# Folding 40 of 48 adaLN weight tiles on VectorE, with one partition sum on TensorE for each group of eight

## The reference

```python
def adaln(cond, w, b):
    m = jax.nn.silu(cond) @ w + b
    return jnp.split(m[..., None, :], 6, axis=-1)
# per layer: adaln(c, w_ada[l], b_ada[l]) for the latents, adaln(c_ctx, w_ada[l], b_ada[l]) for the context
# w_ada[l] is (1024, 6144)
```

## Time and profile before

| | |
|---|---|
| time, median of 3 runs | 1704.29 us (1699.11 to 1709.53) |
| span of the profiled execution | 1699.1 us |
| TensorE busy | 1617.3 us, 95% |
| VectorE busy | 522.5 us, 31% |
| ScalarE busy | 316.4 us, 19% |
| 48 adaLN tiles on TensorE (L1033) | 55.5 us |

### The profile page before, as it was taken

How to read it: one execution, slowest core, us unless ns; L and a number is a source line. 1 busy time by engine, 2 the same in 40 slices (tenths; PEclk the granted TensorE clock), 3 DMA queues, 4 the chain that set the end, 5 groups by cost and what they waited for, 6 DMA issues and landing times.

```text
span 1699.1 us, 21403 instructions
## 1 busy us (share of the span) xinstructions
PE 1617.3 (95%) x9009; PEld 987.5 (58%) x9009; DVE 522.5 (31%) x1217; ACT 316.4 (19%) x715; POOL 64.8 (4%) x68
## 2 busy tenths in 40 slices
PE   5999998999999999989999989999999998899987
PEld 2665644744444436854546556786678887555543
DVE  1232365522332212441211115345534314211112
ACT  2121234211111100110101013234312201100001
POOL 0000000000000000020000013000000000100000
PEclk8999999999999999999999999999999999999999
DMA  9564412232424348179999995422123466999996
GB/s 368 191 223 149 149 38 82 56 112 90 170 87 173 136 139 307 61 242 398 420 393 407 393 375 193 126 94 75 38 97 127 135 236 267 346 393 387 399 383 264
DMA packets 118863, 370.52 MB, mean 218 GB/s; under 512 B 6722, under 2 KB 83580, under 8 KB 96236
## 3 DMA queue, kind: packets, MB, share of 16 engines
q1 hardware_dynamic: 109516, 344.70, 54.4%
q0 software_dynamic: 4400, 13.69, 2.4%
q10 hardware_dynamic: 4848, 10.73, 2.0%
HBM read 356.40 MB, written 12.69 MB: 217 GB/s over the span
## 4 chain that ended last, share of the span: by engine, by line
PE 83%; DMA 5%; DVE 4%; ACT 2%; SPq 2%; issue 2%; another core or an unknown queue 1%; POOL 1%; ACTq 0%; DVEq 0%; POOLq 0%
PE ps L1223 15%; PE ps L1363 14%; PE ps L1096 11%; PE ps L1099 9%; PE ps L1020 8%; PE ps L1240 7%; PE ps L1381 6%; PE ps L1033 3%; DMA ring<-in_w_exp_gate 3%; SPq L852 2%; PE ps L1131 1%; PE ps L1126 1%; PE ps L1353 1%; PE ps L1406 1%
## 5 line engine op out<-in xcount | busy, mean ns | idle before, releaser
L1223 PE MATMUL ps<-hT,ring 128*128 128x512 f32 (+1 forms) x768 | 262.2, 491 | 1.4 <-ACT arena L1650 1.4
L1096 PE MATMUL ps<-hT,ring 128*128 128x512 f32 (+1 forms) x544 | 210.3, 540 | 0.0
L1223 PEld LDWEIGHTS ps<-hT,ring 128*128 128x128 f32 x768 | 142.4, 190 | 115.3 <-issue 105.9
L1099 PE MATMUL ps<-ring,hT 128*128 128x256 f32 (+1 forms) x832 | 174.5, 367 | 5.1 <-DVE arena L1926 4.0
L1099 PEld LDWEIGHTS ps<-ring,hT 128*128 128x128 f32 x832 | 147.4, 191 | 35.9 <-issue 18.7
L1096 PEld LDWEIGHTS ps<-hT,ring 128*128 128x128 f32 x544 | 101.4, 191 | 98.2 <-issue 93.2
L1240 PE MATMUL ps<-arena,ring 128*128 128x512 f32 (+1 forms) x384 | 133.4, 487 | 0.0
L1363 PE MATMUL ps<-ring,arena 128*64 128x256 f32 (+2 forms) x928 | 118.2, 378 | 8.3 <-DMA ring<-in_w_exp_gate 3.0
L1363 PE MATMUL ps<-arena 128*64 128x256 f32 (+2 forms) x1008 | 99.6, 355 | 2.7 <-DMA arena<-in_w_exp_up 1.7
L1240 PEld LDWEIGHTS ps<-arena,ring 128*128 128x128 f32 x384 | 72.2, 190 | 51.6 <-issue 46.7
L1363 PEld LDWEIGHTS ps<-ring,arena 128*64 128x64 f32 (+2 forms) x928 | 68.0, 136 | 55.3 <-issue 36.0
(11 more groups left out here) (265 smaller groups left out, 1531.8 us busy)
## 6 DMA issues: line engine op xcount, KB each, us to landing
ring<-in_w_in SPq DMA_DIRECT2D x54, 1024.0 KB, 6.3
ring<-in_w_ada SPq DMA_DIRECT2D x48, 1024.0 KB, 7.1
arena<-in_w_exp_down SPq DMA_DIRECT2D x18, 2048.0 KB
arena<-in_w_exp_up SPq DMA_DIRECT2D x15, 2048.0 KB, 25.4
ring<-in_w_exp_down SPq DMA_DIRECT2D x14, 2048.0 KB, 24.4
ring<-in_w_exp_gate SPq DMA_DIRECT2D x12, 2048.0 KB, 24.3
ring<-in_w_exp_up SPq DMA_DIRECT2D x12, 2048.0 KB, 24.9
hT<-in_w_exp_gate SPq DMA_DIRECT2D x10, 2048.0 KB, 24.9
```

The costliest lines, as they stand in the source:

```text
L1096: last = pe.matmul(ps[:, bank, 0:tok.stop - tok.start], w[:, k, at:at + width], hT[:, k, tok], start=(k == 0), stop=(k == KD - 1))
L1099: last = pe.matmul(ps[:, bank, 0:width], hT[:, k, P * tok:P * (tok + 1)], w[:, k, at:at + width], start=(k == 0), stop=(k == KD - 1))
L1223: last = pe.matmul(ps[:, 0, lo:TOK], kview(n)[:, k, P * (m % 2):P * (m % 2 + 1)], hT[:, k, lo:TOK], start=(k == 0), stop=(k == KD - 1))
```

## The change

Forty tiles no longer go to TensorE. `fold` scales a tile on VectorE by the condition's value of each row (a scalar for each partition) and adds it to an accumulator of 128 x 2048, one for each condition. After eight tiles `ada_sum` sums the accumulator over the partitions with four matmuls a condition, whose stationary operand `cond_row` holds one column of ones. The context condition is left out where nothing reads it (groups 1 and 2 of layer 1). The accumulators lie in parts of the arena and of the retention table that are free at that time. A slot of the ring is now given back by the last `fold` of its tile. The first eight tiles stay as they are. Some semaphores are merged and GpSimd sets `cond_row` at the start.

```diff
+def folded_conds(l, g):
+    return (0, 1) if first_tile(l) == 0 or g == 0 else (1,)
...
+        folded = ((region(8192, 2048), region(10240, 2048)), (region(12288, 2048), ret_flat[:, 0:2048]))
...
                 if l == 0:
-                    for _ in range(ada_after(n) - ada_after(n - 1)):
-                        add(0.858, "ada", 0, next(ada))
                     for g in range(1, ADA_GROUPS):
                         if ada_after(n - 2) < KD * (g + 1) <= ada_after(n - 1):
+                            add(1.75, "ada_sum", 0, g)
                             add(0, "modulation", 0, g)
+                    for _ in range(ada_after(n) - ada_after(n - 1)):
+                        j = next(ada)
+                        for cnd in folded_conds(0, j // KD):
+                            add(0, "fold", 0, j, cnd)
...
+                    if to_sum is not None:
+                        add(0.86 * len(folded_conds(l + 1, to_sum)), "ada_sum", l + 1, to_sum)
+                        add(0, "modulation", l + 1, to_sum)
+                        to_sum = None
                     for k in range(KD):
                         add(us(q_cols), "gate", v, k)
+                    if l + 1 < DEPTH:
+                        j = next(ada)
+                        for cnd in folded_conds(l + 1, j // KD):
+                            add(0, "fold", l + 1, j, cnd)
+                        to_sum = j // KD if j % KD == KD - 1 else None
...
-                        j = next(ada)
-                        add(0.858, "ada", l + 1, j)
-                        if j % KD == KD - 1:
-                            add(0, "modulation", l + 1, j // KD)
...
             if kind == "ada":
-                return ada_ready, ADA_TILES * l + j + 1
+                return (ada_ready, j + 1) if l == 0 and j < DIRECT else (ada_folded[1], folds(l, j + 1, 1))
...
+            def ada_sum(l, g):
+                pe.wait_ge(mods_row, ADA_GROUPS * l + g)
+                if g == 1:
+                    pe.wait_ge(mods_a, l + 1)
+                pe.wait_ge(rows_zeroed, 7)
+                conds = folded_conds(l, g)
+                for cnd in conds:
+                    pe.wait_ge(ada_folded[cnd], folds(l, KD * (g + 1), cnd))
+                    for c in range(4):
+                        last = pe.matmul(ps[32 * c:32 * (c + 1), 7, :], cond_row[:, cnd, :], folded[l][cnd][:, 512 * c:512 * (c + 1)],
+                                         start=(cnd == conds[0]), stop=(cnd == 1))
+                last.then_inc(ada_ready, 1)
...
+            def fold(l, j, cnd):
+                g, k = divmod(j, KD)
+                n, acc = place[("ada", l, j)], folded[l][cnd]
+                arrived(dve, n)
+                if k == 0:
+                    dve.wait_ge(ada_ready, sums(l, g))
+                    ins = dve.tensor_scalar(acc, slot(n), cond[:, k, cnd:cnd + 1], None, ALU.mult)
+                else:
+                    dve.wait_ge(ada_folded[cnd], folds(l, j, cnd))
+                    ins = dve.scalar_tensor_tensor(out=acc, in0=slot(n), scalar=cond[:, k, cnd:cnd + 1], in1=acc,
+                                                   op0=ALU.mult, op1=ALU.add)
+                ins.then_inc(ada_folded[cnd], 1)
```

More of the change, by code:

```diff
@@ L623, in mixer_plan @@
             g_begins = at
-            ada = iter(range(ADA_TILES))
+            ada, to_sum = iter(range(ADA_TILES)), None
             for b_n, b in enumerate(BRANCH_ORDER):
@@ L640, in mixer_plan @@
                             add(0, "keep_mods", l + 1)
-                        j = next(ada)
-                        add(0.858, "ada", l + 1, j)
-                        if j % KD == KD - 1:
-                            add(0, "modulation", l + 1, j // KD)
+            if to_sum is not None:
+                add(0.86, "ada_sum", l + 1, to_sum)
+                add(0, "modulation", l + 1, to_sum)
             nc, nb, na = (sum(u[0] == kind for u in units[l]) for kind in "cba")
@@ L734, in multiplied, with folds, sums @@
             return (moe.gate, moe.up, moe.down)[j], EXPERTS * l + max(i for i in range(EXPERTS) if i % WAYS[l][j] == 0) + 1
+        def folds(l, j, cnd):
+            own = lambda m, upto: sum(cnd in folded_conds(m, n // KD) for n in range(DIRECT if m == 0 else 0, upto))
+            return sum(own(m, ADA_TILES) for m in range(l)) + own(l, j)
+        def sums(l, g):
+            return DIRECT + ADA_GROUPS * l + g - DIRECT // KD
         def cap_of(l, i):
@@ L889, in _ @@
                         sp.wait_ge(moe.summed, NT)
-                        sp.wait_ge(ada_ready, ADA_TILES * (l + 1))
+                        sp.wait_ge(ada_ready, sums(l, ADA_GROUPS))
                         sp.dma_start(ret_c, ret_consts.rearrange("p (a u) -> p a u", a=4)).then_inc(ret_in, 16)
@@ L1023, in ada_tile @@
             def ada_tile(l, j):
[L1025 to L1030 removed]
+                k, n = j % KD, place[("ada", l, j)]
                 arrived(pe, n)
@@ L1263, in _ @@
                         branch(*at)
-                    elif what == "ada":
-                        ada_tile(*at)
+                    elif what == "ada_sum":
+                        ada_sum(*at)
                     elif what == "mods_turn":
@@ L1532, in squares @@
                    .then_inc(std_ready, 1)
-            act.wait_ge(eps_set, 1)
+            act.wait_ge(consts_made, 1)
             def tile_done(l, i):
@@ L1852, in modulation @@
                     dve.wait_ge(bias_in[min(g, 1)], 32 if g else 96)
-                dve.wait_ge(ada_ready, ADA_TILES * l + KD * (g + 1))
+                dve.wait_ge(ada_ready, sums(l, g + 1))
                 row = mod_rows(l, g)[:, 0, :]
@@ L2115, in _ @@
                         table(*at)
+                    elif what == "fold":
+                        fold(*at)
                     elif what == "modulation":
@@ L2411, in _ @@
             pool.memset(mod_rows(0, 1, 2), 0).then_inc(rows_zeroed, 1)
-            pool.memset(zero_i[:, :], 0).then_inc(list_set, 1)
-            pool.iota(tok_i[:, :], pattern=[[P, NT]], base=0, channel_multiplier=1).then_inc(list_set, 1)
-            pool.wait_ge(list_set, 1)
+            pool.memset(cond_row[:, :, :], 0).then_inc(rows_zeroed, 1)
+            pool.wait_ge(rows_zeroed, 5)
+            for cnd in range(2):
+                pool.memset(cond_row[:, cnd, cnd:cnd + 1], 1.0).then_inc(rows_zeroed, 1)
+            pool.memset(zero_i[:, :], 0).then_inc(rows_zeroed, 1)
+            pool.iota(tok_i[:, :], pattern=[[P, NT]], base=0, channel_multiplier=1).then_inc(rows_zeroed, 1)
+            pool.wait_ge(rows_zeroed, 8)
             pool.dma_start(list_d.rearrange("(p n) o -> p (n o)", p=P), zero_i[:, :]).then_inc(zeroed, 16)
-            pool.wait_ge(list_set, 2)
+            pool.wait_ge(rows_zeroed, 9)
             pool.wait_ge(zeroed, 16)
```

31 lines of the change are left out of this document (13 added, 18 removed).

## The result

The changed kernel takes 1677.5 us (median of 4 runs, 1676.61 to 1679.77) and the kernel before 1703.42 (4 runs, 1699.11 to 1709.53): ratio 0.985, 95% interval 0.983 to 0.9869. It is faster by 1.5%, and 1677.0 was predicted. In a later set of runs the changed kernel had 0.9838 (0.9821 to 0.9855). Its profiled execution has a span of 1675.5 us and a time of 1677.15, so 1.65 us lie around the span.

The account below looks back on a forecast made before the run. TensorE, busy 95% of the span, was taken to bound the kernel. Gains of 0.8 (through the c units), 5.1 (b units) and 21.7 (gates) sum to 27.6 us, taking the median from 1704.3 to 1677; range 1663 to 1694.

Parts of the forecast that it names:

- What leaves, what comes, the folds: Tiles free TensorE of 38.9 us, sums add 7.6, net 31.3; on VectorE a fold takes 2.35, a first scale 1.28.
- Rival 5: Slower: folds run at the strided operation's 3.7 to 3.9 us; 1720 us at 3.9; chance 0.06.
- Stage 1: From 68.4 us to the first sum: folds just fit, up to 1 us lost; TensorE done at 126.2, not 133.6.
- Stage 2: Layer 0's c units: saves 7.4 us, loses 14.0 to waits and half clock; lead at unit 9 about 0.8.
- Stage 3, "+7.0 - 1.9 = 5.1": Layer 0's b units: new order at unit 18 saves 7.0 us of wait and clock, second sum costs 1.9.
- The 2.9 us for half clock behind a long wait: TensorE in layer 0: 2.9 us added behind the 4.0 us wait, half behind the 2.8, 2.9 saved at unit 18.
- Stage 4, "24.0 - 3.9 + 1.65": Gate stage: 24 tiles at 1.00 us leave, sums cost 3.9, a 1.65 wait goes; gain 21.7 us.
- Nothing waits: Gate stage: VectorE's one or two folds a step, 2.4 or 4.8 us, fit in 13.1 us; no wait.
- starts earlier as a whole: Output projection and experts: the whole lead of 27.6 us carries through, their transfers being released earlier too.
- 3's mechanism: Unit 18's order doesn't help, or more long waits lower the clock: gain 9 to 20 us, 1684 to 1695; chance 0.23.
- rival 2: No waits from folds, or folds near 2.2 us: gain 34 to 40 us, down to 1664; chance 0.15.

Follow-up runs that it names:

- e3: Changed kernel with the four folds of a pair of layer 0's tiles spread over the next projection tile's matmuls; 1669.1 us, ratio 0.9798.
- e1: Kernel before with ScalarE's seven transfers moved behind the exponentials of unit 18; 1697.04 us, ratio 0.9968.
- e8: Changed kernel run and profiled once more, unchanged; 1674.39 us, ratio 0.9838 to the kernel before.
- e5: Kernel before run and profiled once more, unchanged; 1699.97 us (one run).
- e4: Changed kernel with the planned times of layer 0's projection, so the order of units, as in the kernel before; 1673.53 us, ratio 0.9819 to the kernel before.
- e9: Changed kernel with layer 0's 16 tiles back on TensorE and the seven transfers behind unit 18's exponentials; 1674.53 us, ratio 0.9818 to the kernel before.
- e10: Kernel of e7 with every layer 0 unit's division right behind its exponentials; 1671.62 us, ratio 0.9812 to the kernel before.
- e7: Changed kernel with the edits of e1, e3 and e4 together; 1663.53 us, ratio 0.9781 to the kernel before.
- e11: Kernel of e7 with the division right behind the exponentials for units 8 to 15 alone; 1661.88 us, ratio 0.9766 to the kernel before.
- e12: Kernel of e7 once more, unchanged; 1662.32 us, ratio 0.9773 to the kernel before.

## Why the prediction was right, and where its steps were not

**What leaves, what comes, the folds.** The net of 31.3 us of TensorE work (31.2 measured), the fold of 2.35 (2.346) and the scale of 1.28 (1.280) held. The Trainium skill ("VectorE: DVE Perf Modes", the perf-mode tier table) gives 2293 ns for a `tensor_tensor` of 2048 fp32 elements. A fold is a `scalar_tensor_tensor`, also with two tensor operands; the trace has 2346 for it, and the sum was right to keep its own. Rival 5 is excluded by that row.

**Stage 1** held: 126.62 for 126.2. No TensorE wait there was longer than the 0.31 us at 103.7.

**Stage 2** was charged too much and credited too much. "Stage 2 saves 8 tiles, 7.4" is a miscount: of layer 0's 16 tiles ten stood ahead of 133.6 (their 9.3 less the first sum's 1.9 is the 7.4 of stage 1) and six behind it, so 5.6. With the right count the forecast would have been 25.8. Against that the waits were 0.56, 3.42 and 2.37, 6.4 us instead of 9.6 (the 0.54 at 182 is in before too), and the clock cost 1.7 instead of 4.4. So 2.8 us of lead were lost, not 6.6. The two long waits stand where the walk had them. e3 shows the mechanism: spread, the same folds cause neither.

**Stage 3, "+7.0 - 1.9 = 5.1", is the step that failed.** The 7.0 is real (e1: 7.1 against the same profile). What was missed is that the shifted times moved the units against the jobs all along the list. Leaving out the wait of 3.0 us that both have, before waited 0.95, 0.22, 1.34 and 4.61, together 7.1 us; after waits 0.61, 0.99, 0.73, 2.20, 0.37, 0.66 and 1.61, together 7.2. Unit for unit, 0.73 (unit 14), 0.86 more at unit 15, 0.37 (unit 17) and 1.61 (a job) are new, 3.6 us in all, and the 2.20 drew the clock down for about 1.6 us: that is the 5.2 between 5.1 and the -0.1 of the first pair of profiles. In the second pair the stage gave -3.2, since the clock fell elsewhere: behind the first transposes of e8 it cost 1.6 us more than in after, and behind the wait at unit 18 in e5 1.3 less than in before. e4 has the old order and the same gate, and the four waits at units 14, 15 and 17 and at the job are as in before; but part of its lead was won ahead of the b units, so it shows the worth of the order for both stages together. The prediction compared ScalarE's order at one unit, and not where the jobs of the other units end.

The 2.9 us for half clock behind a long wait was too much as a rule. Behind the 4.61 us it was 2.7 in the profile that it was read from, and 1.4 in e5. Behind the 3.00 us at 235.47 before lost 3.0 us by it, e5 1.6; yet both came to the transposes two units on at the same distance, 17.6 and 17.5 us (253.04 and 253.30), because before then waited 0.22 us and e5 1.60.

**Stage 4, "24.0 - 3.9 + 1.65", was mis-sized** by 4.0: 25.7 instead of 21.7. "Nothing waits" held for TensorE: VectorE waited 11.7 us for tiles of the ring in four times, and nobody waited for it. The term that was wrong is the 1.00 us a tile, read off the tile's own row; its pitch is 1.19. From the groups, 2.0 us of gate matmuls and 0.3 of branch matmuls went with the tiles, beside 25.6 of the tiles less 4.3 of the sums and the wait of 1.65: 25.3 of the 25.7.

**Behind the gates, "starts earlier as a whole",** failed by 6.2 us in the first pair of profiles and by 3.5 in the second. The stretch to layer 1's projection took 415.9 before and 420.4 after. Waits of PE by what ended them, in this stretch, after and then e5:

```profile
PE ps L1417 <- issue: 8.2, 4, 3.3
PE ps L1417 <- DMA arena<-in_w_exp_down: 2.0, 1, 2.0
```
```profile
PE ps L1381 <- issue: 4.4, 2, 3.5
PE ps L1381 <- DMA arena<-in_w_exp_down: 1.7, 1, 1.7
```

The down projections of the experts wait longer. The profile puts most of it down to "issue", that is, to nothing that it shows, but two of these waits in after end when weights land: the transfers that SP issued at 929.32 and 947.25 took 29.6 and 30.7 us, and the matmuls began at 958.96 and 978.08. Time from issue to landing of all the down projection's weights of this stretch, after and then before:

```profile
DMA to landing us min/median/max: 13.1/27.4/32.2
```
```profile
DMA to landing us min/median/max: 12.9/24.4/27.3
```

Over fourteen profiles the stretch took 412.8 to 417.8 us where the output projection began above 651 (four), and 416.2 to 421.5 where it began below 634 (ten), with no order among these ten (417.8 at 616.8, 421.5 at 631.6). So some 3 us are given back on the mean when TensorE comes early. The landing time goes with it: the median is 27.4 to 27.8 us in the four profiles whose stretch is over 420 (after, e8, e9, e10) and 24.1 to 26.8 in the ten others. Why these weights land later was not isolated. It is neither layer 0's folding (e9) nor arrival time alone.

**The sum came out** because errors cancelled. In the first pair of profiles stages 1 and 2 were 3.4 us better than walked, stage 3 was 5.2 worse, stage 4 4.0 better, and what follows 6.2 worse: 23.6 instead of 27.6. The medians differ by 25.9. In the second pair the stages add up to 22.3 with other terms (3.3, -3.2, 25.7 and -3.5). That the median lies within 1 us of the forecast is luck. Of the rivals, 3's mechanism (more waits in the b units) was there, inside the forecast's range; rival 2's 1664 was reached only by e7 (and e11, built on it), which takes the waits away.

## What to carry to other kernels

Work moved to an idle engine costs what it delays, not what it takes: 9.1 us of folds in one block ahead of a copy cost two long waits and a half clock, and the same folds one by one cost three shorter waits and no half clock. When a planner's times shift, compare every engine's list at every unit, not only at the place that improves, and look also for steps that keep their order and move by one matmul: a gain of 7 us was paid for by four small waits, a half clock and the second sum. Price a removed matmul stretch by the pitch of whole steps with and without it, not by its own row.

## What the runs showed of the hardware that was not expected

- **The clock is not a function of the wait.** In layer 0's c and b units the waits of 2.98 us and above on transposes or outputs were followed by half clock in each profile, but the six matmuls behind the one near 236 took 7.41 us in e1 and 6.06 in e5, a difference of 1.4. Waits of 1.93 and 1.94 in two executions of one kernel were followed by 5.42 and by 7.11 us, 2.37 by a granted clock of 1.00 and of 0.83, and the 2.85 in e10 by none that shows. The Trainium skill ("TensorE: Matmul & The Clock Gate", Part 1) says of the start of a kernel that the cost of a cold array varies from run to run; these pairs show the same in the middle of one.
- **A half clock ahead of another wait can cost nothing.** e12 lost 1.7 us by it that e7 did not lose, and before 1.4 more than e5, and in both pairs the next wait was shorter by about as much (1.50 for 0.45 and 2.67; 0.22 for 1.60).
- **32-column matmuls lengthen their neighbours.** A tile alone costs 1.19 us of a step and shows 1.00; the full-width groups on either side bear the rest: 7.13 us for the 16 gate records beside tiles, 7.03 without. Two tiles together pay it once.
- **The same weights land later in kernels that differ only up to the output projection.** From issue to landing the down projection's weights take 24.4 and 24.3 us (median) in the two profiles of before, and 27.4 and 27.8 in those of after, at a DMA share of 1.01 to 1.02 around them.
